# Routing steps of a mixture-of-experts kernel: low parts issued ahead of the wait for a step's end

## What is computed

```
q   = x @ peer_wq                      # 8 heads x 256
s1  = q[:, :128] @ keys1.T             # 128 scores a half
s2  = q[:, 128:] @ keys2.T
v1, i1 = top_k(s1, 16); v2, i2 = top_k(s2, 16)
c   = v1[:, None] + v2[None, :]        # 256 candidates
v, p = top_k(c, 16)
expert = i1[p // 16] * 128 + i2[p % 16]
gate = softmax(v)
out = sum over all experts of gate * gelu(x @ u) * v_expert
```

## Time and profile before

| | us |
|---|---|
| median of 3 runs | 2506.39 (2502.34 to 2509.07) |
| the profiled execution | 2505.94 |
| its span, first to last instruction | 2504.1 |
| TensorE busy | 2412.5 (96%) |
| VectorE busy | 1748.9 (70%) |
| ScalarE busy | 1343.7 (54%) |
| GpSimd busy | 709.0 (28%) |

### The profile page before, as it was taken

How to read it: one execution, slowest core, us unless ns; L and a number is a source line. 1 busy time by engine, 2 the same in 40 slices (tenths; PEclk the granted TensorE clock), 3 DMA queues, 4 the chain that set the end, 5 groups by cost and what they waited for, 6 DMA issues and landing times. The chain is left out here.

```text
span 2504.1 us, 57329 instructions
## 1 busy us (share of the span) xinstructions
PE 2412.5 (96%) x16509; PEld 2211.3 (88%) x16509; DVE 1748.9 (70%) x3945; ACT 1343.7 (54%) x2396; POOL 709.0 (28%) x564
## 2 busy tenths in 40 slices
PE   6999999999999999999999999999999999899998
PEld 6899999999888888889999999988888887688996
DVE  5647777887677777554777788777777767556346
ACT  3545555776555555454555567655555543444443
POOL 5665444000000000566544400000000043134665
PEclk9999999999999999999999999999999999999999
DMA  6244566444566666623466644456666644333554
GB/s 239 85 153 168 210 230 226 168 152 180 177 245 236 246 236 243 237 85 137 167 217 225 228 164 161 174 182 241 241 241 242 243 157 158 142 135 110 174 186 152
DMA packets 98053, 475.31 MB, mean 190 GB/s; under 512 B 11808, under 2 KB 13344, under 8 KB 50720
## 3 DMA queue, kind: packets, MB, share of 16 engines
q1 hardware_dynamic: 97392, 472.91, 53.3%
q10 hardware_dynamic: 560, 1.19, 0.1%
HBM read 438.41 MB, written 35.65 MB: 189 GB/s over the span
## 5 line engine op out<-in xcount | busy, mean ns | idle before, releaser
L1415 ACT ACTIVATE wh<-ring 128x512 fp32r<-128x512 f32 x1428 | 881.9, 627 | 613.9 <-ACTq L1414 609.3
L2103 DVE TENSOR_TENSOR wl<-ring,wh 128x512 fp32r<-128x512 f32 x961 | 674.1, 707 | 273.0 <-DVEq L2102 254.2
L1100 PE MATMUL PS<-xh,wh 128*128 128x256 f32 x2048 | 593.6, 290 | 9.7 <-PEq L1096 8.2
L1100 PE MATMUL PS<-xl,wh 128*128 128x256 f32 x2048 | 579.6, 283 | 0.0
L1100 PE MATMUL PS<-xh,wl 128*128 128x256 f32 x2048 | 579.5, 283 | 0.0
L510 POOL TENSOR_TENSOR wl<-ring,wh 128x512 fp32r<-128x512 f32 x295 | 390.8, 1349 | 289.1 <-POOLq L509 287.3
L895 PE MATMUL PS<-wh,xh 128*128 128x512 f32 x1088 | 425.2, 391 | 2.5 <-PEq L892 2.5
L895 PE MATMUL PS<-wh,xl 128*128 128x512 f32 x1088 | 423.5, 389 | 0.0
L895 PE MATMUL PS<-wl,xh 128*128 128x512 f32 x1088 | 423.3, 389 | 0.0
L1100 PEld LDWEIGHTS PS<-xh,wh 128*128 128x128 f32 x2048 | 392.3, 192 | 15.3 <-issue 14.6
L1100 PEld LDWEIGHTS PS<-xl,wh 128*128 128x128 f32 x2048 | 392.9, 192 | 0.0
(11 more groups left out here) (339 smaller groups left out, 3826.5 us busy)
## 6 DMA issues: line engine op xcount, KB each, us to landing
ring<-in_peer_u SPq DMA_DIRECT2D x128, 1024.0 KB, 4.8
ring<-in_peer_v SPq DMA_DIRECT2D x128, 1024.0 KB, 4.8
acts<-stg SPq DMA_DIRECT2D x124, 256.0 KB, 2.1
gains<-acts SPq DMA_DIRECT2D x124, 256.0 KB, 4.9
ring<-in_w_in SPq DMA_DIRECT2D x24, 1024.0 KB, 4.9
ring<-in_w_gate_up SPq DMA_DIRECT2D x22, 1024.0 KB, 4.8
ring<-in_peer_wq SPq DMA_DIRECT2D x16, 1024.0 KB, 4.8
ring<-in_w_down SPq DMA_DIRECT2D x11, 1024.0 KB, 4.9
```

The source lines that it names most:

```text
L1100: last = pe.matmul(PS[:, 2 * j, 0:S], w[:, q, k * P:(k + 1) * P], x[:, at, :], start=at + i == 0, stop=at + i == 9)
L1415: act.activation(wh[:, q, :], ring[:, s, q * QW:(q + 1) * QW], ACT.Copy).then_inc(high_ready[q], 1)
L2103: part = dve.tensor_tensor(wl[:, q, :], ring[:, s, q * QW:(q + 1) * QW], wh[:, q, :].bitcast(F32), SUB)
```

## The change

`own` is split into `mark` (the increment on the step's last instruction itself, so that the `engine_nop`s go) and `settle` (the wait). A low part of the routing is written between the two. Parts of quarter 3 have no wait of their own now (`low_odd`): `parts_ready[3]` is given by the instruction itself, and the slot is released by `freed` behind a later `settle`. The difference to the best (`shifted`) moves from the end of the pass to beside the index parts. The last part of a pass, quarter 3 of D, keeps the old form.

```diff
-                def best_keys(c, s, beside=None):
+                def mark(ins):
+                    ins.then_inc(dve_own, 1)
+
+                def settle():
+                    dve.wait_ge(dve_own, 1)
+                    dve.sem_inc(dve_own, -1)
+
+                def low_odd(k):
+
+                    s, q = k // 2 % 2, 2 * (k % 2) + 1
+                    dve.wait_ge(high_ready[q], 1)
+                    dve.sem_inc(high_ready[q], -1)
+                    dve.tensor_tensor(wl[:, q, :], ring[:, s, q * QW:(q + 1) * QW], wh[:, q, :].bitcast(F32),
+                                      SUB).then_inc(parts_ready[q], 1)
+
+                def freed(k):
+                    dve.sem_inc(chunk_free[k // 2 % 2], 1)
+
+                def best_keys(c, s, lows=False):
                     dve.wait_ge(scores_ready, 1)
                     dve.sem_inc(scores_ready, -1)
                     for a in range(4):
-                        dve.max(s16c[:, a, 0:8], scc[s][:, a, :])
-                    own(dve.engine_nop())
-                    if beside:
-                        beside(0)
+                        last = dve.max(s16c[:, a, 0:8], scc[s][:, a, :])
+                    mark(last)
+                    if lows:
+                        low_odd(0)
+                    settle()
                     for a in range(4):
                         dve.max_index(i16c[:, a, 0:8], s16c[:, a, 0:8], scc[s][:, a, :])
-                        dve.match_replace(scr[:, a, :], s16c[:, a, 0:8], scc[s][:, a, :], -3e38)
-                    own(dve.engine_nop())
-                    if beside:
-                        beside(1)
+                        last = dve.match_replace(scr[:, a, :], s16c[:, a, 0:8], scc[s][:, a, :], -3e38)
+                    mark(last)
+                    if lows:
+                        low_odd(1)
+                    settle()
                     for a in range(4):
-                        dve.max(s16c[:, a, 8:16], scr[:, a, :])
-                    own(dve.engine_nop())
-                    if beside:
-                        beside(2)
+                        last = dve.max(s16c[:, a, 8:16], scr[:, a, :])
+                    mark(last)
+                    if lows:
+                        low_odd(2)
+                    settle()
+                    if lows:
+                        freed(1)
                     for a in range(4):
-                        dve.max_index(i16c[:, a, 8:16], s16c[:, a, 8:16], scr[:, a, :])
-                    own(dve.engine_nop())
-                    if beside:
-                        beside(3)
+                        last = dve.max_index(i16c[:, a, 8:16], s16c[:, a, 8:16], scr[:, a, :])
+                    mark(last)
+                    if lows:
+                        low_odd(3)
+                    settle()
                     dve.tensor_copy(s16[:, c, :], s16c[:, :, :].rearrange("p a k -> p (a k)"))
                     own(dve.tensor_copy(i16[:, c, :], i16c[:, :, :].rearrange("p a k -> p (a k)")))
+                    if lows:
+                        freed(3)
                     dve.sem_inc(scores_used, 1)
 
                 with dve.Fori(0, N_WQ // 2 - 1) as i:
                     for s in (0, 1):
                         best_keys(2 * i + s, s)
-                def low_odd(k):
-                    low(k // 2 % 2, 2 * (k % 2) + 1)
 
                 dve.wait_ge(pool_lows_done, 1)
                 dve.sem_inc(pool_lows_done, -1)
-                best_keys(N_WQ - 2, 0, low_odd)
-                best_keys(N_WQ - 1, 1, low_odd)
+                best_keys(N_WQ - 2, 0, True)
+                best_keys(N_WQ - 1, 1, True)
...
+                    def shifted(t):
+                        dve.tensor_scalar(sel[:, 2, t, bass.ts(c, TOPK)], t16[:, TOPK * t:TOPK * t + TOPK],
+                                          t16[:, TOPK * t:TOPK * t + 1], None, SUB)
 
...
+                    mark(last)
                     low_odd(0)
+                    settle()
+                    mark(best(0, cand))
+                    low_odd(1)
+                    settle()
                     for t in range(TT):
                         k = TOPK * t
                         dve.max_index(p16[:, k:k + 8], t16[:, k:k + 8], cand[:, t, :])
-                        dve.match_replace(candr[:, t, :], t16[:, k:k + 8], cand[:, t, :], -3e38)
-                    own(dve.engine_nop())
-                    low_odd(1)
-                    best(8, candr)
+                        last = dve.match_replace(candr[:, t, :], t16[:, k:k + 8], cand[:, t, :], -3e38)
+                    mark(last)
+                    low_odd(2)
+                    settle()
+                    freed(1)
+                    mark(best(8, candr))
+                    settle()
                     for t in range(TT):
                         k = TOPK * t + 8
-                        dve.max_index(p16[:, k:k + 8], t16[:, k:k + 8], candr[:, t, :])
-                    own(dve.engine_nop())
-                    low_odd(2)
+                        last = dve.max_index(p16[:, k:k + 8], t16[:, k:k + 8], candr[:, t, :])
+                    mark(last)
+                    low_odd(3)
+                    settle()
                     dve.tensor_scalar(pj[:, 0, :], p16[:, :], 4, None, ALU.logical_shift_right)
-                    own(dve.tensor_scalar(pj[:, 1, :], p16[:, :], 15, None, ALU.bitwise_and))
-                    own(dve.tensor_copy(pf[:, :, :], pj[:, :, :]))
-                    is_one(0)
-                    low_odd(3)
-                    pick(0)
-                    picked(0)
+                    mark(dve.tensor_scalar(pj[:, 1, :], p16[:, :], 15, None, ALU.bitwise_and))
+                    shifted(0)
+                    settle()
+                    freed(3)
+                    mark(dve.tensor_copy(pf[:, :, :], pj[:, :, :]))
+                    shifted(1)
+                    settle()
+                    mark(is_one(0))
                     low_odd(4)
-                    is_one(1)
-                    pick(1)
+                    settle()
+                    mark(pick(0))
+                    settle()
+                    mark(picked(0))
                     low_odd(5)
-                    picked(1)
+                    settle()
+                    mark(is_one(1))
+                    settle()
+                    freed(5)
+                    mark(pick(1))
                     low_odd(6)
-                    for t in range(TT):
-                        dve.tensor_scalar(sel[:, 2, t, bass.ts(c, TOPK)], t16[:, TOPK * t:TOPK * t + TOPK],
-                                          t16[:, TOPK * t:TOPK * t + 1], None, SUB)
-                    own(dve.engine_nop())
-                    low_odd(7)
+                    settle()
+                    mark(picked(1))
+                    settle()
+                    low(1, 3)
```

More of the change, by code:

```diff
@@ L2418, in is_one @@
                     def is_one(a):
-                        own(dve.tensor_tensor(oneh[:, :, :], bc(iota16[:, :].unsqueeze(1), TT * TOPK, TOPK),
-                                              bc(pf[:, a, :].unsqueeze(2), TT * TOPK, TOPK), ALU.is_equal))
+                        return dve.tensor_tensor(oneh[:, :, :], bc(iota16[:, :].unsqueeze(1), TT * TOPK, TOPK),
+                                                 bc(pf[:, a, :].unsqueeze(2), TT * TOPK, TOPK), ALU.is_equal)
                     def pick(a):
@@ L2424, in pick @@
                             x = oneh[:, TOPK * t:TOPK * t + TOPK, :]
-                            dve.tensor_tensor(x, x, bc(iv[:, t, a, :].unsqueeze(1), TOPK, TOPK), MUL)
-                        own(dve.engine_nop())
+                            last = dve.tensor_tensor(x, x, bc(iv[:, t, a, :].unsqueeze(1), TOPK, TOPK), MUL)
+                        return last
                     def picked(a):
-                        own(dve.tensor_reduce(sel[:, a, :, bass.ts(c, TOPK)],
-                                              oneh[:, :, :].rearrange("p (t k) j -> p t k j", t=TT), AX.X, ADD))
+                        return dve.tensor_reduce(sel[:, a, :, bass.ts(c, TOPK)],
+                                                 oneh[:, :, :].rearrange("p (t k) j -> p t k j", t=TT), AX.X, ADD)
                     def best(at, src):
                         for t in range(TT):
-                            dve.max(t16[:, TOPK * t + at:TOPK * t + at + 8], src[:, t, :])
-                        own(dve.engine_nop())
-                    for t in range(TT):
-                        dve.tensor_tensor(cand[:, t, :].rearrange("p (i j) -> p i j", i=TOPK),
-                                          bc(sv[:, t, 0, :].unsqueeze(2), TOPK, TOPK),
-                                          bc(sv[:, t, 1, :].unsqueeze(1), TOPK, TOPK), ADD)
-                    own(dve.engine_nop())
-                    best(0, cand)
+                            last = dve.max(t16[:, TOPK * t + at:TOPK * t + at + 8], src[:, t, :])
+                        return last
+                    def shifted(t):
```

(19 more changed lines are left out.)

## The result

| | before | changed |
|---|---|---|
| median, us (4 runs each, taken together) | 2507.59 | 2539.03 |
| lowest to highest | 2502.34 to 2509.07 | 2535.92 to 2543.10 |
| ratio, 95% interval | | 1.013 [1.0116, 1.0143] |
| the profiled execution, its span | 2505.94, 2504.1 | 2535.92, 2533.9 |

The change makes the kernel slower by 1.3%. The forecast was 2528 us, in a range of 2506 to 2536: the direction is right, the size too small, and the median lies 3 us above the range.

A forecast was written before the change was run, and what follows sets the result against it. TensorE was taken to bound the routing passes; passes of 25.0 us add 22.0, the chunks before the loop 1.2, and the start gives back 0.6. That makes +22.6 on 2506.39, stated as 2528 us, range 2506 to 2536.

The forecast's parts named there:

- A's start: A, B, C, D are the four chunks of one routing-loop pass; times count from TensorE's start of A.
- TensorE bounds the passes, and a load must go out within 4.23: Routing passes: TensorE isn't held if a load goes out within 4.23 us of the slot's previous chunk's start.
- A's release goes behind B's second quarter: the load at 4.91, C at 12.20: Routing loop: A's later release sends C's load at 4.91 us, so C starts at 12.20 instead of 11.52.
- rival 4: Releases wait for the part's end: 0.65 us more a pass, +10, 2538 us; chance 0.11.
- VectorE and GpSimd collide on C: Routing pass: after C's late load, VectorE and GpSimd exclude each other on two-input steps, delaying C's second and fourth quarters.
- GpSimd's part of D at 14.85: GpSimd works on D's quarter 0 from 14.85 to 16.1 us, delaying C's fourth quarter to 16.0.
- C's load 5.5 after C, the next A 12.8 after C, a pass of 25.0: C's slot, released behind the one-hot step, makes the next A late; sixteen passes of 25.0 us give +22.0.
- The four chunks before the loop have one release of A's kind ... +1.2: Four chunks ahead of the loop: 12.2 us instead of 11.62 and 11.53, +1.2 us.
- the start gives back 0.6: One wait less, 0.3 us, before the first chunk's second quarter in each layer: 0.6 us back.
- Rival 1: Only C's load is late, VectorE and GpSimd don't meet: passes of 23.75 us, 2509 us; chance 0.13.
- rival 2: TensorE sets the pace: C's load goes out by 4.2 us after A, gaps close, 2497 us; chance 0.11.
- Rival 3: The change doesn't make VectorE faster: passes of 24.0 us, +6 + 1.2, 2513 us; chance 0.05.

The follow-up runs named there:

- experiment 7: Changed kernel with only A's slot in the loop released right behind its part by an engine_nop, all else late: 2510.33 us, ratio 1.002.
- experiment 5: Changed kernel with every slot released right behind its fourth quarter by engine_nop, and D's second quarter ahead of the second pick: 2497.68 us, ratio 0.9969.
- experiment 8: Changed kernel with only C's slot in the loop released right behind its part, all else late: 2530.9 us, ratio 1.0097.
- Experiment 2: best_keys of the changed kernel with the loop of the kernel before: 2513.53 us, ratio 1.0029.
- experiment 9: Changed kernel with A's slot in the loop and chunk 0's in best_keys released at once by engine_nop, other changed releases late: 2502.36 us, ratio 0.999.
- experiment 3: best_keys of the kernel before with the loop of the changed kernel: 2538.94 us, ratio 1.0125.
- experiment 4: Kernel before with only A's release in the loop moved behind B's second quarter: 2540.28 us, ratio 1.013.
- experiment 1: Changed kernel with every slot released right behind its fourth quarter's part by an engine_nop, same order of parts: 2503.76 us, ratio 0.9988.

## Why the prediction was right and wrong

By its own steps, with A's start as 0:

- *TensorE bounds the passes, and a load must go out within 4.23.* Right as far as it was tried: with C's load at 4.09 to 4.28 no next A waits (experiment 7), and with A's at 4.77 C is late. With all loads in time and D's part ahead of the pick (experiment 5) a pass is 23.04. But the loads aren't all that can hold TensorE back, see the fourth step.
- *A's release goes behind B's second quarter: the load at 4.91, C at 12.20.* Right: 4.77 and 12.21 in the pass shown, 12.03 to 12.73 but for two passes. The release ran 0.39 behind the start of a part of 0.83; rival 4 (it waits for the end) is out, though its 2538 us is near the measured time, by luck.
- *VectorE and GpSimd collide on C.* Right in kind, wrong in place. C's second quarter ended 12.61 after A (12.6 predicted). The fourth was to be blocked by GpSimd's part of D at 14.85; that part came at 15.87, since I let D's load land after 5.05, and behind C's late load it took 6.0. The block fell on the second pick instead, and the stall on D's second quarter. The rows show what such a block cost: the pick took 2.54 and the one-hot step 1.78 beside GpSimd's parts, 0.76 and 0.68 alone. It isn't only steps with two inputs that GpSimd blocks, as the prediction has it: its own rows at 325.34 (1.27) and 337.03 (1.40) are steps that read one tensor.
- *C's load 5.5 after C, the next A 12.8 after C, a pass of 25.0.* This path was wrong. C's load goes out at 4.68 or 4.69 in fourteen of the sixteen passes, and the next A comes 12.30 to 12.43 after C in thirteen. It waits for no load there: D's second quarter, behind the blocked second pick, stalls TensorE by 0.65 to 0.88 in fourteen passes, and the prediction doesn't follow that part. With C's load at 3.95 it still comes at 12.30 and later (experiment 8). Only the pass with 5.78 and 13.60 goes the forecast way. That the sum of both loops came out near, +21.1 where +22.0 was forecast, is in good part luck.
- *"The four chunks before the loop have one release of A's kind ... +1.2", and "the start gives back 0.6".* **This step failed.** I priced the stretch of the earlier trace rows that begins with chunk 2, and left out that chunk 0's slot has a release of the same kind: `freed(1)` stands in each of the two calls of `best_keys` that serve chunks. +5.4 came in place of these +0.6. Experiment 2 has it alone, +6.8; experiment 9 takes it away. A part of it is a cost that I had nowhere, 1.7 us: in the changed kernel both layers have 3.4 us at half clock here, in the kernel before one of them.
- *The rest.* +1.3 ahead of the expert stages, -2.5 between and +4.3 behind them were not forecast. The last is four stalls of 0.9 to 1.2 us ahead of L870, in a loop that the change doesn't touch; the second trace of the changed kernel has none of the four. The median lies another 3.1 above the profiled execution.
- *The sums.* 2506.39 + 22.6 is 2529.0, not 2528, and C's load with a release that waits goes out at 5.65, not 5.56 (4.48 + 0.69 + 0.48). Neither matters for the outcome.
- *Rival 1* (no collision) and *rival 2* (faster) are out by the loads at 4.77 and by the blocked steps. *Rival 3*, VectorE isn't faster, is out too: the part of 340.83 starts 0.60 behind the start of a step of 0.69, while behind a wait the idle time alone is 0.23 to 0.33.

The range was drawn round the passes, its upper end 8 us above the forecast. It had no room for the chunks ahead, nor for passes of two kinds: experiment 3 has eleven passes over 25.2 us, the changed kernel four. The changed kernel's own runs spread over 7 us. Whether its slower runs have more long passes is open: the two traces, of 2535.92 and 2533.33 us, have four each. Open as well: what D's second quarter ahead of the second pick would save with the releases left late, which no run has; whether the time behind the second expert stage has to do with the change at all (854.0 and 854.2 in the two traces of the kernel before, 852.7 to 860.6 in all others), and why some first passes of experiment 4 took 28.3.

## What to carry to other kernels

When a step moves in a queue, list what it *releases* and to whom, count every place with that pattern, and compare each release with the latest time that its consumer allows: 0.5 us past the limit cost more here than all the saved waits could give. Then follow every part that stands behind a step that can be held up, not only the one whose release moves. A release can stay where it was while the wait goes: an increment on an empty instruction behind the last reader did it here (the load went out 0.27 us behind the part's end), and the saved waits then showed (2503.76 and 2497.68 us in experiments 1 and 5). Where two engines hold each other up, as VectorE's pick and GpSimd's part did here (1.85 instead of 0.76), put what TensorE waits for ahead of the long shared step.

## What the runs showed of the hardware

- A semaphore step of VectorE's queue ran while the instruction ahead was under way: the load went out 0.25 and 0.39 us behind the start of parts of 0.69 and 0.83. An increment on an empty instruction came behind the part's end: in experiment 1 a part of 0.69 starts at 316.64 and the load goes out at 317.60, 0.27 behind its end, where the old form with its own wait took 0.48.
- GpSimd's waiting part went in between two steps that stand next to each other on VectorE: the two products of the second pick took 1.11 and 1.51, 2.54 together, where both take 0.76 alone, and GpSimd's two parts of 341.48 took 3.23 together, where one takes 1.30 alone. In the two passes shown GpSimd's part of D comes 3.66 and 3.03 after C's start, and the passes take 24.51 and 25.63.
- Two loads of 1 MB on one queue, issued 4.12 us apart, didn't land 4.12 apart: in layer 1 of the changed kernel the second took 5.2 to 6.9, and about 4.8 in the kernel before, where loads are 4.5 apart or more.
- A stall of TensorE was followed by half its clock in some places and not in others: experiment 2 has the stalls ahead of the passes in layer 2 at clock 1.00, and experiment 9 has idle stretches of 1.7 to 2.4 us in both expert stages, all at 1.00. In both traces of the kernel before and in several others the granted clock fell to 0.50 for 3.4 us behind an idle stretch of TensorE of 1.8 to 2.7 us, here in experiment 1 behind the one-hot matmuls that follow the passes:

```profile
451.60:455.00 3.40, 2.04 (x10) 1.81 (x9) 0.50 0.07 29
```

The rest of that expert stage took 215.22 instead of 213.65. Both layers of experiments 1 and 5 lose 1.6 to 1.9 us in this way, and the gain of their passes doesn't show in full.
